# Recurrent gates as three split products of high and low parts, in place of two full fp32 products

## The reference

```
u = causal_depthwise_conv(u, conv_w, conv_b)          # four taps per channel
ub = uf.reshape(B, S, LRU_BLOCKS, LRU_BLOCK_DIM)      # 16 blocks of 64 channels
r = sigmoid(einsum('bshi,hij->bshj', ub, w_rg) + b_rg)
i = sigmoid(einsum('bshi,hij->bshj', ub, w_ig) + b_ig)
log_a = -LRU_C * r * softplus(-lru_lambda)
a = exp(log_a)
xin = sqrt(-expm1(2 * log_a)) * (i * uf)
h_t = a_t * h_{t-1} + xin_t                            # associative scan
```

## Time and profile before

| | |
|---|---|
| median of three runs | 2716.71 us |
| span of the profiled execution | 2716.7 us |
| TensorE busy | 2684.2 us, 99% |
| VectorE busy | 1636.0 us, 60% |
| ScalarE busy | 1023.7 us, 38% |
| fp32 gate products in all | 16, between 64 and 141 us |

### The profile page before, as it was taken

The page is one execution under the profiler, slowest core; times in us unless marked ns, Lnnn a source line. Parts: engine busy times, 40 slices in busy tenths (PEclk is TensorE's granted clock), DMA queues, the critical chain, the costliest instruction groups (busy, mean ns, idle before and its releaser), DMA issues.

```text
span 2716.7 us, 35226 instructions
## 1 busy us (share of the span) xinstructions
PE 2684.2 (99%) x14493; PEld 2206.2 (81%) x14493; DVE 1636.0 (60%) x3271; ACT 1023.7 (38%) x1749; POOL 14.1 (1%) x43
## 2 busy tenths in 40 slices
PE   8999999999999999999999999999999999999999
PEld 5788888889888888766888889888889676888888
DVE  7766555357767556777776746763346777633334
ACT  4642332445222244665422224222234565422223
POOL 1000000000000000000000000000000000000000
PEclk9999999999999999999999999999999999999999
DMA  8255334133655334411555524643223510232331
GB/s 253 92 172 170 112 93 117 63 109 110 216 186 186 109 110 118 128 32 33 185 186 186 188 91 140 194 144 96 93 93 116 141 54 32 66 106 93 98 100 66
DMA packets 345352, 331.41 MB, mean 122 GB/s; under 512 B 11362, under 2 KB 334694, under 8 KB 345192
## 3 DMA queue, kind: packets, MB, share of 16 engines
q1 hardware_dynamic: 344820, 328.62, 38.9%
q10 hardware_dynamic: 372, 0.55, 0.1%
HBM read 320.74 MB, written 2.10 MB: 119 GB/s over the span
## 4 chain that ended last, share of the span: by engine, by line
PE 94%; DVE 4%; ACT 1%; DMA 0%; SPq 0%; issue 0%; DVEq 0%
PE bank L542 26%; PE bank L544 26%; PE bank L543 26%; PE bank L584 3%; PE bank L570 2%; PE bank L2410 2%; PE bank L572 2%; PE bank L571 2%; PE bank L2439 1%; PE bank L1388 1%; PE bank L1378 1%; PE bank L2042 1%; DVE w_lo L510 1%; DMA mw<-in_w_mod 0%; PE bank L867 0%; DVE E L2534 0%
## 5 line engine op out<-in xcount | busy, mean ns | idle before, releaser
L542 PE MATMUL bank<-h_lo,w_hi 128*128 128x512 f32 (+1 forms) x2448 | 924.9, 378 | 3.6 <-DVE h_lo L709 2.2
L544 PE MATMUL bank<-h_hi,w_lo 128*128 128x512 f32 (+1 forms) x2448 | 900.7, 368 | 0.0
L543 PE MATMUL bank<-h_hi,w_hi 128*128 128x512 f32 (+1 forms) x2448 | 899.1, 367 | 0.0
L510 DVE TENSOR_TENSOR w_lo<-raw,w_hi 128x1024 fp32r<-128x1024 f32 (+1 forms) x422 | 490.9, 1200 | 314.9 <-ACT w_hi L504 314.7
L504 ACT ACTIVATE w_hi<-raw 128x1024 fp32r<-128x1024 f32 (+1 forms) x422 | 421.5, 1035 | 345.9 <-PE bank L544 328.2
L542 PEld LDWEIGHTS bank<-h_lo,w_hi 128*128 128x128 f32 x2448 | 461.9, 189 | 87.9 <-issue 8.0
L543 PEld LDWEIGHTS bank<-h_hi,w_hi 128*128 128x128 f32 x2448 | 462.3, 189 | 77.2 <-issue 5.1
L544 PEld LDWEIGHTS bank<-h_hi,w_lo 128*128 128x128 f32 x2448 | 460.9, 188 | 77.9
L542 PE MATMUL bank<-a_lo,w_hi 128*128 128x512 f32 (+1 forms) x1056 | 390.8, 370 | 0.0
L544 PE MATMUL bank<-a_hi,w_lo 128*128 128x512 f32 (+1 forms) x1056 | 384.6, 364 | 0.0
L543 PE MATMUL bank<-a_hi,w_hi 128*128 128x512 f32 (+1 forms) x1056 | 384.0, 364 | 0.0
(11 more groups left out here) (315 smaller groups left out, 2529.8 us busy)
## 6 DMA issues: line engine op xcount, KB each, us to landing
swf<-in_w_ada SPq DMA_DIRECT2D x60, 1024.0 KB, 7.9
raw<-in_ffn_w_gate SPq DMA_DIRECT2D x44, 1024.0 KB, 5.4
raw<-in_ffn_w_up SPq DMA_DIRECT2D x44, 1024.0 KB, 5.4
raw<-in_w_in SPq DMA_DIRECT2D x40, 1024.0 KB, 5.1
raw<-in_ffn_w_down SPq DMA_DIRECT2D x32, 1024.0 KB, 5.2
raw<-in_w_in SPq DMA_DIRECT2D x34, 512.0 KB, 5.1
raw<-in_ffn_w_down SPq DMA_DIRECT2D x16, 768.0 KB, 4.6
mw<-in_w_mod SPq DMA_DIRECT2D x8, 1024.0 KB, 11.7
```

The lines of the kernel that those rows point to most:

```text
L510: nc.vector.tensor_tensor(o, r, half(w_his[place_of[i]], i, h)[0].bitcast(F32), ALU.subtract).then_inc(*w_lo.up((i, h)))
L542: nc.tensor.matmul(o, w1, al, start=start, stop=False)
L543: nc.tensor.matmul(o, w1, ah, start=False, stop=False)
L544: return nc.tensor.matmul(o, w2, ah, start=False, stop=stop)
```

## The change

The gate products take the same three-product form as the dense ones. That needs high and low parts of the gate weights (once) and of every block of `uc`:

- `act_gate_weights` and `dve_gate_weights` make `wg_hi` and `wg_lo` from `wrg` and `wig`. `wg_lo` lies on top of the fp32 weights. They stand behind the U2 conversion of their engine.
- `act_conv_high(p)` copies two blocks of `uc` into `uc_hi`, and `dve_conv_low(p)` makes `uc_lo`. There are two buffers of each.
- On ScalarE the copies of pair 0 stand behind the copies of `u` blocks 2 and 3; those of pair p + 1 stand behind `act_decay(p)`.
- On VectorE the subtractions of pair 0 stand behind the convolution of block 2 and ahead of that of block 3; those of pair p + 1 stand behind `dve_decay(p)`.
- `pe_gates_of(c)` waits for `wg_lo` and for the low part of block c; before, it waited for the loaded weights and the convolution of c.
- `dve_conv(c)` waits for the high and low parts of block c - 4 in place of the gate products.
- The scratch that the program sets aside for dynamic DMA is set to 2048 bytes, and the new tiles need 16 KB more of each partition.

```
     def pe_gates_of(c):
         br, bi = bank(("br", c), B_AUX), bank(("bi", c), B_AUX)
-        pe.wait_ge(ld_wg, 0)
-        pe.wait_ge(dve, ("conv", c))
-        nc.tensor.matmul(br[:, :], wrg[:, c * 128:c * 128 + 128], uc[c % 4][:, :], start=True, stop=True)
-        nc.tensor.matmul(bi[:, :], wig[:, c * 128:c * 128 + 128], uc[c % 4][:, :], start=True, stop=True)
+        pe.wait_ge(dve, "wg_lo")
+        pe.wait_ge(dve, ("cl", c))
+        for t, key, o in ((br, "br", 0), (bi, "bi", 1024)):
+            cols = slice(o + c * 128, o + c * 128 + 128)
+            three(t[:, :], wg_hi[:, cols], wg_lo[:, cols], uc_lo[c % 2][:, :], uc_hi[c % 2][:, :], True, True)
+    def act_gate_weights():
+        act.wait_ge(ld_wg, 0)
+        for n, t in enumerate((wrg, wig)):
+            nc.scalar.activation(wg_hi[:, n * 1024:n * 1024 + 1024], t[:, :], ACT.Copy)
+    def dve_gate_weights():
+        for n, t in enumerate((wrg, wig)):
+            dve.wait_ge(act, ("wg_hi", n))
+            nc.vector.tensor_tensor(wg_lo[:, cols], t[:, :], wg_hi[:, cols].bitcast(F32), ALU.subtract)
+    def act_conv_high(p):
+        for c in (2 * p, 2 * p + 1):
+            act.wait_ge(dve, ("conv", c))
+            if c >= 2:
+                act.wait_ge(pe, ("bi", c - 2))
+            nc.scalar.activation(uc_hi[c % 2][:, :], uc[c % 4][:, :], ACT.Copy)
+    def dve_conv_low(p):
+        for c in (2 * p, 2 * p + 1):
+            dve.wait_ge(act, ("ch", c))
+            if c >= 2:
+                dve.wait_ge(pe, ("bi", c - 2))
+            nc.vector.tensor_tensor(uc_lo[c % 2][:, :], uc[c % 4][:, :], uc_hi[c % 2][:, :].bitcast(F32), ALU.subtract)
@@ act_recurrent
         act_w(("U", 2), 0)
+        act_gate_weights()
         for c in (2, 3):
             act_u(c)
+        act_conv_high(0)
         act_w(("L", 1), 0, 0)
         act_gates_of(0)
         act_w(("L", 1), 0)
         act_decay(0)
+        act_conv_high(1)
...
             act_decay(p)
+            act_conv_high(p + 1)
@@ dve_recurrent
         dve_w(("U", 2), 0)
+        dve_gate_weights()
         dve_conv(2)
+        dve_conv_low(0)
         dve_conv(3)
...
         dve_decay(0)
+        dve_conv_low(1)
...
             dve_decay(p)
+            dve_conv_low(p + 1)
```

More of the change, by code:

```diff
@@ L330, in carve, with here @@
         place = [start]
-        def here(name, cols):
-            t = sb(name, cols, at=place[0])
+        def here(name, cols, dt=F32, over=0):
+            place[0] -= over
+            t = sb(name, cols, dt, at=place[0])
             place[0] += (cols * 4 + 63) // 64 * 64
@@ L357, in build @@
     wrg, wig = here("wrg", 1024), here("wig", 1024)
+    wg_lo = here("wg_lo", 2048, F32R, 8192)
+    wg_hi = here("wg_hi", 2048, F32R)
+    uc_hi, uc_lo = ([here(f"{n}{i}", 512, F32R) for i in range(2)] for n in ("uc_hi", "uc_lo"))
     here = carve(phase1)
@@ L1061, in pe_gates_of @@
         br, bi = bank(("br", c), B_AUX), bank(("bi", c), B_AUX)
-        pe.wait_ge(ld_wg, 0)
-        pe.wait_ge(dve, ("conv", c))
[L1064 to L1067, removed]
+        pe.wait_ge(dve, "wg_lo")
+        pe.wait_ge(dve, ("cl", c))
+        for t, key, o in ((br, "br", 0), (bi, "bi", 1024)):
+            cols = slice(o + c * 128, o + c * 128 + 128)
+            three(t[:, :], wg_hi[:, cols], wg_lo[:, cols], uc_lo[c % 2][:, :], uc_hi[c % 2][:, :], True, True).then_inc(
+                *pe.up((key, c)))
+    def act_gate_weights():
+        act.wait_ge(ld_wg, 0)
+        for n, t in enumerate((wrg, wig)):
+            nc.scalar.activation(wg_hi[:, n * 1024:n * 1024 + 1024], t[:, :], ACT.Copy).then_inc(*act.up(("wg_hi", n)))
+    def dve_gate_weights():
+        for n, t in enumerate((wrg, wig)):
+            cols = slice(n * 1024, n * 1024 + 1024)
+            dve.wait_ge(act, ("wg_hi", n))
+            nc.vector.tensor_tensor(wg_lo[:, cols], t[:, :], wg_hi[:, cols].bitcast(F32), ALU.subtract).then_inc(
+                *dve.up("wg_lo" if n else ("wg_lo", 0)))
+    def act_conv_high(p):
[3 more added lines that the diff above has]
+                act.wait_ge(pe, ("bi", c - 2))
+            nc.scalar.activation(uc_hi[c % 2][:, :], uc[c % 4][:, :], ACT.Copy).then_inc(*act.up(("ch", c)))
+    def dve_conv_low(p):
[3 more added lines that the diff above has]
+                dve.wait_ge(pe, ("bi", c - 2))
+            nc.vector.tensor_tensor(uc_lo[c % 2][:, :], uc[c % 4][:, :], uc_hi[c % 2][:, :].bitcast(F32), ALU.subtract).then_inc(
+                *dve.up(("cl", c)))
     def act_u(c):
@@ L1120, in dve_conv @@
         if c >= 4:
-            dve.wait_ge(pe, ("bi", c - 4))
+            dve.wait_ge(act, ("ch", c - 4))
+            dve.wait_ge(dve, ("cl", c - 4))
             dve.wait_ge(dve, ("iu", c - 4))
@@ L3211 @@
     arrays.update(host_constants())
-    nc = program(lambda: _bacc.Bacc("TRN2", target_bir_lowering=False, num_devices=1),
+    nc = program(lambda: _bacc.Bacc("TRN2", target_bir_lowering=False, num_devices=1, dynamic_dma_scratch_size=2048),
                  {n: a.shape for n, a in arrays.items()})
```

## The result

The changed kernel took 2737.33 us, the median of four runs (2735.33 to 2738.58), against 2717.36 us of the kernel before (2716.07 to 2718.75). The ratio is 1.0071, with a 95% interval of 1.0059 to 1.0083: 20 us slower, where 17.6 were forecast.

A forecast was written before the change was run, and what follows sets the result against it. TensorE was taken as the bound, its delays reaching the end one for one: 2716.7 - 2.5 (products) + 8.5 + 8.2 (waits) + 3.4 (clock) = 2734.3 us. The 8 in 10 range was 2729.5 to 2739.

The forecast's parts named there:

- What bounds the kernel: Whole kernel: TensorE, busy 2684.2 of 2716.7 us; its gains or losses between 64 and 141 us reach the end one for one.
- The products: Gate products on TensorE: three split products replace one fp32, saving 0.36 us a block in seven blocks, 2.5 us.
- The first wait: Gates of block 0: TensorE waits for the low part behind VectorE's queue, from 64.48 to 73.0, 8.5 us.
- Blocks 2 to 5 without a wait: Gates of blocks 2 to 5: low parts come in time, with a 5 us margin for 4 and 5.
- The second wait: Gate 6: the low part stands behind pair 2's decay; TensorE arrives at 137.3 and resumes at 145.5, 8.2 us.
- The clock: Behind both 8 us waits TensorE runs at half clock, losing 1.7 us each, 3.4 us in all, range 0 to 6.8.
- the two nearest cases: Start of the kernel: waits of 2.1 and 3.6 us, each with 3.4 us at low clock, 1.7 us lost.
- The sum against its own base: Whole kernel: terms added to the 2716.7 us span, taken as equal to the median 2716.71 with nothing around it.
- A: Rival on the gates: low parts arrive in time, only the 2.5 us saving is seen, 2714.2 us; chance 4%.
- B: Rival at gate 6: the second wait is covered by slack in pair 2's chain, 2724.4 us; chance 7%.
- C: Rival: VectorE's lag also makes gate 4 or pb0's low parts late, costing 2 to 4 us, 2737.5 us; chance 9%.
- added lag: Ahead of block 6's convolution: two high parts on ScalarE and the second low part delay it by 1.2 us.

The follow-up runs named there:

- kernel 1: Kernel before with its gate products in three-product form on operands that are there anyway, no split or wait added; 2715.24 us, ratio 0.9988.
- kernel 9: Changed kernel with only the gate weights' split moved ahead of L0's weights on ScalarE and VectorE; 2735.37 us in one run.
- Kernel 2: Changed kernel with gate weights split ahead of L0's weights and block 0 split right after its convolution, block 1 after U2's weights; 2726.55 us, ratio 1.0030.
- kernel 5: Changed kernel with 32 extra products, results overwritten, ahead of TensorE's waits at gate 0 and gate 6; 2734.64 us, ratio 1.0053.
- kernel 6: Changed kernel with TensorE's order alone altered: both blocks' gate products stand behind the second block of the L unit; 2723.81 us, ratio 1.0019.
- Kernel 4: Changed kernel with the order altered around both the first and the second wait, all its work kept; 2718.47 us, ratio 0.9999.
- 8: Kernel 4 plus ten and fourteen unused identity transposes ahead of two TensorE waits in the first 25 us; 2717.98 us, ratio 0.9995.
- 3: Changed kernel with splits in pairs 2 and 3 made earlier, low parts ahead of the decay; 2729.24 us, ratio 1.0040.
- 7: Changed kernel with all splits and waits, but each gate product again one fp32 product of the high parts; 2740.27 us, ratio 1.0077.

## Why the prediction was right

**What bounds the kernel.** Right. The 18.6 us of the stage are found at the end but for what the clock gives and takes.

**The products.** Right in sign and about in size: 2.5 us forecast, 2.8 in kernel 1's stage.

**The first wait.** Forecast 8.5, measured 8.45. Every term of the sum over VectorE's queue has its row above, and kernel 9 confirms one by taking it out. The point where the wait ends was forecast as 73.0 and was 73.65, since this execution had started 0.6 us later. The profile counts a wait from the modelled end of the product before it; from start to start, as the forecast counted, the two waits are 8.6 and 8.4 us, so both were forecast some 0.1 to 0.2 us short.

**Blocks 2 to 5 without a wait.** Right: the list of waits has only the two.

**The second wait.** Forecast 8.2, measured 8.24. What carried it was to see that the stretch from 85.64 us is ScalarE's and VectorE's own, so that a delay of TensorE moves it along instead of using up its lead. Kernel 2 shows it: there TensorE comes to gate 6 some 10 us earlier and still waits 8.24 us. The wait ended at 148.29 and not at the 145.5 of the forecast, because the later start (0.6) and what the clock took behind the first wait (2.0) moved this stretch as well.

**The clock.** The mechanism was right, and this is the term that was mis-sized: 3.4 us forecast, 4.3 measured, and 4.0 in the stage by kernel 5. The low level held for 10.2 us over each wait and what follows, of which 4.0 and 4.5 us met work, more than the 3.4 us of the two nearest cases. By the Trainium skill (TensorE: Matmul & The Clock Gate, section "HAM oscillation — how this bites in real kernels"), a TensorE that waits for data long enough starts its next stretch at half rate. The traces agree behind both waits of 8 us (granted clock 0.50), and with kernel 5, where the gaps are filled and the clock is 1.00. Behind shorter waits they agree only at times, as told below.

**The sum against its own base.** One step failed: that nothing lies around the span because 2716.7 equals the median. The profiled run of the kernel after took 2735.33 us with a span of 2734.0, so 1.3 us lie around the span, and the run profiled before was not the median one. Put right, the forecast is 2735.6 for such a run; it took 2735.33. The agreement is in part luck, since 1.8 us came back behind the stage, against the clock's 0.9 and a start that was 0.5 us later. The profiled run is also the fastest of the four, 2.0 us below their median of 2737.33; the others were not traced, and where their 1.2 to 3.3 us more lie is not shown.

**The rivals.** A (low parts in time) and B (one wait) are refuted by the two waits. A third wait (C) isn't there. The last exponential of pair 2 started at 146.28 against 134.28, 12.0 us later: 0.6 of start, 8.15 of the first wait, 2.0 of clock, and the 1.2 us of added lag that the forecast counted.

## What to carry to other kernels

A cheaper instruction on the bounding engine is worth its saving only if its operands are there as early as those of the old one. Before splitting an operand, count what stands in the producer's queue ahead of the new piece, at every place where it is used: 2.5 us of faster products were paid for with 17 us of waits and 4 of clock, and the same work in another order had none of them. Even then the gain, 1.8 us of the stage, could not be told from nothing in the medians. When TensorE has to wait several microseconds, add what the clock takes behind the wait (1.7 to 3.0 us behind each wait of 6 to 8 us in these kernels); products put into the gap took 4.0 of 4.3 us back in kernel 5.

## What the runs showed of the hardware

**The same wait may or may not cost clock.** In kernel 6, waits of 3.0 and 2.9 us were followed by about 6 us of work at half clock and by none. The wait for the transfer of `mw`, which ends near 24 us, takes 3.63 us both in the kernel before and in the kernel after, and the clock of 24 to 30 us is 0.72 in the one and 1.00 in the other. A wait's price in clock is a range, not a number.

**Stretches at the low clock come and go far from the change.** The 1.8 us behind the stage lie near 2160 us, where the kernel after has one stretch less at the low level. Here is the same place in the kernel before and the kernel after (clock 0.91 and 1.00):

```profile
2150.00:2170.00 20.00, 18.68 (x125) 13.34 (x122) 14.13 (x35) 10.09 (x26) 0.00 (x0) 0.91 0.68 188
```
```profile
2168.00:2188.00 20.00, 18.67 (x141) 13.53 (x140) 15.01 (x39) 9.92 (x27) 0.00 (x0) 1.00 0.71 198
```

Before, 0.09 x 20 / 0.5 = 3.6 us at the low level, after none, with the same code. Kernel 4 has four such windows of 10 us at 0.83 behind its stage, the first of them one that the kernel before does not have, which is where its 1.1 us went:

```profile
1120.00:1130.00 10.00, 9.02 (x39) 6.31 (x37) 8.00 (x25) 4.12 (x12) 0.00 (x0) 0.83 0.85 235
1175.00:1185.00 10.00, 8.93 (x58) 6.46 (x57) 5.87 (x22) 4.01 (x15) 0.00 (x0) 0.83 0.00 2
2155.00:2165.00 10.00, 9.01 (x40) 6.22 (x41) 7.77 (x25) 4.72 (x14) 0.00 (x0) 0.83 0.85 242
2210.00:2220.00 10.00, 8.93 (x55) 6.21 (x53) 5.43 (x20) 4.49 (x14) 0.00 (x0) 0.83 0.01 2
```

Behind the stage TensorE is at the low level in two to four such stretches of about 3.4 us, by windows of 4 us (the last microseconds of the span, where TensorE has nothing left to do, are not counted). The time behind the stage, from the first scores to the end of the span, goes by their number in ten of the eleven profiled executions:

| stretches | kernels | behind the stage, us |
|---|---|---|
| two | the change, 8 | 2414.4, 2414.4 |
| three | before, 1, 6 | 2416.2, 2416.0, 2415.8 |
| four | 2, 3, 4, 5, 7 | 2417.3 to 2417.6 |
| two | 9 | 2416.0 |

So one more goes with some 1.5 us, close to the half of its length that half speed costs, and that is most of what this change could save. Kernel 9 is the exception; it has none near 1197 us, where the kernel after has one, but one near 2177 us, where that has none. What decides whether one comes was not tested.
